# One pass over the sample states, row scaling on ScalarE and a norm on 8 partitions at the end of a gated delta rule

## The reference

```
a_mat = strict_lower((k*beta) k^T * decay);  t_mat = inverse(I + a_mat)
w_v   = t_mat (v*beta);   w_k = t_mat (k*beta*exp(gc))
v_new = w_v - w_k S                       # per chunk, S is the state
o     = (q*exp(gc)) S + (q k^T * decay) v_new
S     = S*g_last + (k*exp(gc_last-gc))^T v_new
o_b   = rms_norm(o, o_norm_w) * silu(g_b)
out   = concat(o_a, o_b) w_out            # 288 tokens x 1024, weights 1024 x 1024
```

## Time and profile before

| | |
|---|---|
| median of 3 runs | 1420.63 us (1409.93 to 1421.68) |
| profiled execution, its own time | 1418.56 us |
| its span, mean granted TensorE clock | 1416.9 us, 0.855 |
| PE busy / DVE / ACT / POOL | 1134.4 / 413.6 / 215.0 / 87.6 us |
| inverse, seven levels | 372.7 to 420.6 us |
| scaling to the last head's output | 420.6 to 485.7 us |
| projection, norm and state update | 485.8 to 541.6 us |
| write of the sample states (L1504) | 2048 KB |

### The profile page before, as it was taken

One profiled execution on the slowest core, in us unless ns is written; L12 is line 12 of the kernel. 1 busy time (PEld: TensorE's weight loads), 2 busy tenths in 40 slices (PEclk: granted clock), 3 DMA queues, 4 the chain that ended last, 5 costly groups with the idle time before them and its releaser, 6 DMA issues. The chain is left out here.

```text
span 1416.9 us, 15651 instructions
## 1 busy us (share of the span) xinstructions
PE 1134.4 (80%) x6028; PEld 611.0 (43%) x6028; DVE 413.6 (29%) x1016; ACT 215.0 (15%) x445; POOL 87.6 (6%) x189
## 2 busy tenths in 40 slices
PE   1999987777778997778788665999999687887755
PEld 0877656564777733325233112444444324222211
DVE  1342234333682243421122113023201521122204
ACT  2221122422000101011011002113101111010001
POOL 6331030040000000000000000000000000000000
PEclk9999968898895577687999877999999688798878
DMA  9251271783600034089999996343423249999991
GB/s 281 69 159 54 60 241 31 212 268 138 251 1 0 1 126 178 1 355 405 397 384 395 392 356 209 105 133 119 156 89 133 105 189 387 420 411 420 383 374 45
DMA packets 87711, 298.73 MB, mean 211 GB/s; under 512 B 16067, under 2 KB 52475, under 8 KB 57902
## 3 DMA queue, kind: packets, MB, share of 16 engines
q1 hardware_dynamic: 67760, 272.91, 50.1%
q0 software_dynamic: 5152, 17.05, 3.9%
q10 hardware_dynamic: 14718, 7.69, 2.0%
HBM read 292.46 MB, written 5.16 MB: 210 GB/s over the span
## 5 line engine op out<-in xcount | busy, mean ns | idle before, releaser
L1052 PE MATMUL ps<-arena,hT 128*32 128x512 f32 x1024 | 142.8, 712 | 93.8 <-DMA arena<-in_moe_w_up 61.1
L1052 PEld LDWEIGHTS ps<-arena,hT 128*32 128x32 f32 x1024 | 38.5, 127 | 187.1 <-issue 187.1
L646 PE MATMUL ps<-hT,arena 128*128 128x288 f32 x448 | 115.2, 420 | 0.0
L1220 PE MATMUL ps<-arena,hT 128*128 128x512 f32 x256 | 114.2, 607 | 0.9 <-ACT hT L1368 0.9
L646 PEld LDWEIGHTS ps<-hT,arena 128*128 128x128 f32 x448 | 87.5, 197 | 27.3 <-issue 1.7
L1220 PEld LDWEIGHTS ps<-arena,hT 128*128 128x128 f32 x256 | 49.5, 195 | 62.7 <-issue 62.6
L2150 DVE TENSOR_TENSOR arena<-ps,arena 128x256 f32<-128x256 f32 x16 | 6.8, 424 | 215.1 <-ACT arena L1551 215.1
L1011 PE MATMUL ps<-htok,arena 128*128 128x512 f32 (+1 forms) x96 | 63.4, 796 | 0.0
L1077 PE MATMUL ps<-arena 128*32 128x512 f32 x512 | 58.2, 595 | 3.3 <-ACT arena L1556 3.3
L1310 PE MATMUL ps<-arena 128*128 128x512 f32 x128 | 59.2, 605 | 0.0
L596 PE MATMUL ps<-ident,htok 128*128 128x128 f32 (+1 forms) x48 | 13.8, 401 | 43.5 <-DVE htok L1654 43.5
(11 more groups left out here) (463 smaller groups left out, 1491.0 us busy)
## 6 DMA issues: line engine op xcount, KB each, us to landing
arena<-in_moe_w_gate SPq DMA_DIRECT2D x66, 1024.0 KB, 12.0
arena<-in_moe_w_up SPq DMA_DIRECT2D x66, 1024.0 KB, 13.2
arena<-in_moe_w_down SPq DMA_DIRECT2D x66, 1024.0 KB, 16.4
arena<-in_cache_k SPq DMA_DIRECT2D x64, 256.0 KB, 3.3
arena<-in_cache_v POOLq DMA_DIRECT2D x64, 256.0 KB, 3.3
arena<-in_w_in_odd SPq DMA_DIRECT2D x16, 1024.0 KB, 10.4
arena<-in_w_in_even SPq DMA_DIRECT2D x14, 1024.0 KB, 10.6
arena<-in_w_out_odd SPq DMA_DIRECT2D x8, 1024.0 KB, 7.0
```

Of the source, the lines that this page charges most:

```text
L646: last = mm(ps[:, c % 4, 0:T], w[:, k, P * (c % 2):P * (c % 2 + 1)], hT[:, k, :], start=k == 0, stop=k == KD - 1)
L1052: last = mm(ps[EC * j:EC * (j + 1), q % 2, :], xgT[:, k, GC * p + EC * j:GC * p + EC * (j + 1)], ring[:, 2 * j:2 * j + 2, DE * k:DE * (k + ...
L1220: last = mm(ps[:, bank, :], hT[:, k, P * i:P * (i + 1)], ring[:, 2 * n:2 * n + 2, QC * k:QC * (k + 1)], start=k == 0, stop=k == KD - 1)
```

## The change

- The last inverse level leaves out the correction of `dT`.
- The row scalings go to ACT, as copies of 128x128 with a scale per row, issued behind its exponentials while the inverse runs; `bex` is made by VectorE ahead of the decay multiplies; buffers `kbe` and `vb` move (v is scaled in place).
- The products with T of tile i write banks 2i and 2i+1; VectorE evicts the first, ACT the second. For the sample tile ACT writes its 4 columns per sample into `wq`, where VectorE puts the decayed q beside them.
- One pass over S0 with 8 columns (`from_states`, bank 5) in two halves of two heads, placed between the steps of the prompt's state chain. Its first 4 columns correct v, the other 4 are added to `oT` by VectorE before the square.
- The heads' prompt part (`o_prompt`) and sample part (`o_sample`) are separate; the transposes of the correction stand between them.
- The sums of squares go to 8 partitions (through `osel`), ACT's root and VectorE's reciprocal work on 8x288, and a product with a column of the identity spreads each head's row to 128 partitions; gate, norm weight and o are multiplied before that.
- `out_proj(j, c)` is one channel block, half of a pair; sums, broadcasts and state products stand between the halves.

```diff
@@ -198,7 +198,10 @@
...
 vdt = htok[:, :, 512:1024].rearrange("p t (h e) -> p t h e", h=HB)
-kbe, vb, wkT, wv = dU, dMT, dT, dLT
+vb, wkT, wv = vdt, dT, dLT
+kbe = wk(4096, 3, HB, P)
+osr = wk(4096, T)
+wq = wk(5632, HB, NB, 2 * QS)
 osq = wk(A + 6144, HB, T)
@@ -604,21 +607,21 @@
...
-    def out_proj(part):
-        for j in part:
+    def out_proj(j, c):
+        if c == 0:
             wait_even(pe, 14 + j)
-            w = cview(14 + j)
...
-                              start=(j == 0 and c == 0), stop=(j == 3 and c == 1))
+        w = cview(14 + j)
+        for i in range(2):
+            for hf in range(2):
+                mm(ps[:, 2 * i + hf, :], mixT[:, 2 * j + c, P * i:P * (i + 1)],
+                   w[:, c, 512 * hf:512 * (hf + 1)],
+                   start=(j == 0 and c == 0), stop=(j == 3 and c == 1))
+        for qr in range(4):
+            last = mm(ps[TS * qr:TS * (qr + 1), 4, 0:QC], mixT[:, 2 * j + c, TP:T],
+                      w[:, c, QC * qr:QC * (qr + 1)],
+                      start=(j == 0 and c == 0), stop=(j == 3 and c == 1))
+        if c == 1:
             last.then_inc(s.w_used, 1)
@@ -862,85 +865,109 @@
...
             for h in range(HB):
-                mm(inv_ps(i, 1)[:, h, :], dTT[0:m, i, h, 0:m], dU[0:m, i, h, 0:m], start=True, stop=True)
+                if l < 6:
+                    mm(inv_ps(i, 1)[:, h, :], dTT[0:m, i, h, 0:m], dU[0:m, i, h, 0:m], start=True, stop=True)
             for h in range(HB):
...
     pe.wait_ge(s.dl_scaled, 2)
-    pe.wait_ge(s.dl_t, 1 + 2 * inv_no(6, 1))
+    pe.wait_ge(s.dl_t, 3 + 2 * inv_no(5, 1))
     for i, (r0, m) in enumerate(TOK):
-        if i:
-            pe.wait_ge(s.dl_w, 2 * i)
         for h in range(HB):
-            mm(ps[0:m, 0, P * h:P * (h + 1)], dTT[0:m, i, h, 0:m], vb[0:m, i, h, :], start=True, stop=True)
+            mm(ps[0:m, 2 * i, P * h:P * (h + 1)], dTT[0:m, i, h, 0:m], vb[0:m, i, h, :], start=True, stop=True)
         for h in range(HB):
-            last = mm(ps[:, 1, P * h:P * h + m], kbe[0:m, i, h, :], dTT[0:m, i, h, 0:m], start=True, stop=True)
+            last = mm(ps[:, 2 * i + 1, P * h:P * h + m], kbe[0:m, i, h, :], dTT[0:m, i, h, 0:m], start=True, stop=True)
         last.then_inc(s.dl_w_ps, 1)
...
+    def state_step(i, bank):
+        for h in range(HB):
+            last = mm(ps[:, bank, P * h:P * (h + 1)], kdt[:, i, h, :], wv[:, i, h, :], start=True, stop=True)
+        last.then_inc(s.dl_s_ps, 1)
+    def from_states(heads):
+        for h in heads:
+            for b in range(NB):
+                last = mm(ps[:, 5, 64 * h + 8 * b:64 * h + 8 * (b + 1)], S0[:, HB * b + h, :], wq[:, h, b, :],
+                          start=True, stop=True)
+        return last
     pe.wait_ge(s.dl_w, 6)
+    state_step(0, 2)
     pe.wait_ge(s.dl_qdec, 1)
-    for h in range(HB):
-        last = mm(ps[:, 2, P * h:P * (h + 1)], kdt[:, 0, h, :], wv[:, 0, h, :], start=True, stop=True)
-    last.then_inc(s.dl_s_ps, 1)
+    pe.wait_ge(s.s0_loaded, 16)
+    from_states((0, 1))
     pe.wait_ge(s.dl_s, 1)
...
     last.then_inc(s.dl_s_ps, 1)
+    from_states((2, 3)).then_inc(s.dl_s_ps, 1)
     pe.wait_ge(s.dl_s, 2)
-    for h in range(HB):
...
-    for h in range(HB):
+    state_step(1, 2)
+    def o_prompt(h):
         b = ps[:, 6 + h % 2, :]
...
             pe.wait_ge(s.dl_o, h - 1)
-        for i, (r0, m) in enumerate(TOK):
-            mm(b[:, r0:r0 + m], wv[0:m, i, h, :], dQK[0:m, i, h, 0:m], start=(i == 0), stop=False,
+        for i in range(2):
+            mm(b[:, P * i:P * (i + 1)], wv[:, i, h, :], dQK[:, i, h, :], start=(i == 0), stop=False,
                skip_group_check=True)
         mm(b[:, P:TP], Sp[:, 0, h, :], cv[:, h, P:TP], start=False, stop=False, skip_group_check=True)
-        for q in range(NB):
...
-    pe.wait_ge(s.dl_osq, 1)
+    def o_sample(h):
+        mm(ps[:, 6 + h % 2, TP:T], wv[0:TS, 2, h, :], dQK[0:TS, 2, h, 0:TS], start=False, stop=True,
+           skip_group_check=True).then_inc(s.dl_o_ps, 1)
+    o_prompt(0)
+    pe.wait_ge(s.dl_s, 3)
     for h in range(HB):
-        if h >= 2:
...
-    pe.wait_ge(s.dl_orms, HB)
+        last = tr(ps[0:TS, 4, P * h:P * (h + 1)], vsT[:, TS * h:TS * (h + 1)], ident[:, :])
+    last.then_inc(s.dl_s_ps, 1)
+    o_prompt(1)
+    pe.wait_ge(s.dl_s, 4)
+    o_sample(0)
+    o_sample(1)
+    for h in (2, 3):
+        o_prompt(h)
+        o_sample(h)
+    def broadcast(h):
+        mm(ps[:, (5, 6, 7, 5)[h], 0:T], bc(ident[0:8, h:h + 1], [8, P]), osr[0:8, :], start=True,
+           stop=True).then_inc(s.dl_oss_ps, 1)
     vx = vexp.rearrange("p b (h e) -> p b h e", h=HB)
-    for j in range(8):
+    def state_change(j):
         h, q = j // 2, j % 2
...
            stop=True).then_inc(s.dl_su_ps, 1)
+    pe.wait_ge(s.dl_st_out, 1)
+    out_proj(0, 0)
+    pe.wait_ge(s.dl_osq, 1)
+    for h in range(HB):
+        last = mm(ps[0:8, 6, 0:T], osel[:, 7 - h:15 - h], osq[:, h, :], start=h == 0, stop=h == HB - 1)
+    last.then_inc(s.dl_oss_ps, 1)
+    out_proj(0, 1)
+    out_proj(1, 0)
+    pe.wait_ge(s.dl_orms, 2)
+    for h in range(3):
+        broadcast(h)
+    out_proj(1, 1)
+    pe.wait_ge(s.dl_mixed, 3)
+    broadcast(3)
+    pe.wait_ge(s.dl_vexp, NB)
+    state_change(0)
+    state_change(1)
     pe.wait_ge(s.dl_mixed, HB)
-    pe.wait_ge(s.dl_su, 8)
-    pe.wait_ge(s.dl_o, HB)
-    out_proj((2, 3))
+    for n in range(4):
+        out_proj(2 + n // 2, n % 2)
+        if n < 3:
+            state_change(2 * n + 2)
+            state_change(2 * n + 3)
@@ -1489,15 +1516,33 @@
...
         A_(dDT[0:m, i, :, 0:m], dDT[0:m, i, :, 0:m], ACT.Exp).then_inc(s.dl_dtx, 1)
+    act.wait_ge(s.dl_scaled, 1)
+    for i in range(3):
+        m = TOK[i][1]
+        for h in range(HB):
+            A_(kbe[0:m, i, h, :], kdt[0:m, i, h, :], ACT.Copy, scale=bex[0:m, i, h:h + 1])
+            A_(vb[0:m, i, h, :], vb[0:m, i, h, :], ACT.Copy, scale=beta[0:m, i, h:h + 1])
+    act.wait_ge(s.dl_cols, 2)
+    for i in range(3):
+        m = TOK[i][1]
+        for h in range(HB):
+            last = A_(kdt[0:m, i, h, :], kdt[0:m, i, h, :], ACT.Copy, scale=kdc[0:m, i, h:h + 1])
+    last.then_inc(s.dl_scaled, 1)
+    for i in range(3):
+        act.wait_ge(s.dl_w_ps, i + 1)
+        src = ps[:, 2 * i + 1, :].rearrange("p (h c) -> p h c", h=HB)
+        if i < 2:
+            A_(wkT[:, i], src, ACT.Copy).then_inc(s.dl_w, 1)
+        else:
+            A_(wq[:, :, :, 0:QS], src[:, :, 0:TS].rearrange("p h (b q) -> p h b q", q=QS), ACT.Copy).then_inc(s.dl_w, 1)
...
         A_(oT[:, h, :], ps[:, 6 + h % 2, 0:T], ACT.Copy).then_inc(s.dl_o, 1)
-    act.wait_ge(s.dl_o, HB)
+    act.wait_ge(s.dl_o, HB + 1)
     A_(osq[:, :, :], oT[:, :, :], ACT.Square).then_inc(s.dl_osq, 1)
-    for h in range(HB):
-        act.wait_ge(s.dl_oss_ps, h + 1)
-        A_(osq[:, h, :], ps[:, 6 + h % 2, 0:T], ACT.Sqrt, scale=1.0 / DB, bias=epsb).then_inc(s.dl_orms, 1)
+    act.wait_ge(s.dl_oss_ps, 1)
+    A_(osr[0:8, :], ps[0:8, 6, 0:T], ACT.Sqrt, scale=1.0 / DB, bias=epsb[0:8]).then_inc(s.dl_orms, 1)
     act.wait_ge(s.dl_st_out, 1)
@@ -1839,6 +1884,8 @@
...
                                    ).then_inc(s.dl_dt, 1)
+    dve.wait_ge(s.dl_cols, 2)
+    V.tensor_tensor(bex, beta, egc, ALU.mult).then_inc(s.dl_scaled, 1)
     for i in range(3):
@@ -1874,50 +1921,38 @@
...
             dve.wait_ge(s.dl_t_ps, inv_no(l, i))
-            V.tensor_tensor(dT[0:m, i, :, 0:m], dT[0:m, i, :, 0:m], inv_ps(i, 1), ALU.subtract)\
-                .then_inc(s.dl_t, 1)
+            if l < 6:
+                V.tensor_tensor(dT[0:m, i, :, 0:m], dT[0:m, i, :, 0:m], inv_ps(i, 1), ALU.subtract)\
+                    .then_inc(s.dl_t, 1)
             V.tensor_tensor(dTT[0:m, i, :, 0:m], dTT[0:m, i, :, 0:m], inv_ps(i, 2), ALU.subtract)\
                 .then_inc(s.dl_t, 1)
-    dve.wait_ge(s.dl_t, 1 + 2 * inv_no(6, 1))
...
-    last.then_inc(s.dl_qdec, 1)
+    dve.wait_ge(s.dl_t, 3 + 2 * inv_no(5, 1))
+    for i in range(2):
+        V.tensor_tensor(cv[:, 0:HB, P * i:P * (i + 1)], cv[:, 0:HB, P * i:P * (i + 1)], eR[:, i], ALU.mult)
+    V.tensor_tensor(wq[:, :, :, QS:2 * QS], cv[:, 0:HB, TP:T].rearrange("p h (b q) -> p h b q", q=QS),
+                    eR[:, 2, :, 0:TS].rearrange("p h (b q) -> p h b q", q=QS), ALU.mult).then_inc(s.dl_qdec, 1)
+    hv = lambda b: ps[:, b, :].rearrange("p (h c) -> p h c", h=HB)
     for i in range(3):
...
         dve.wait_ge(s.dl_w_ps, i + 1)
-        V.tensor_copy(wv[0:m, i], ps[0:m, 0, :].rearrange("p (h c) -> p h c", h=HB)).then_inc(s.dl_w, 1)
...
-    hv = lambda b: ps[:, b, :].rearrange("p (h c) -> p h c", h=HB)
+        V.tensor_copy(wv[0:m, i], hv(2 * i)[0:m]).then_inc(s.dl_w, 1)
+    sq = ps[:, 5, 0:256].rearrange("p (h b c) -> p h b c", h=HB, b=NB)
     dve.wait_ge(s.dl_s_ps, 1)
...
     V.tensor_tensor(wv[:, 1], wv[:, 1], hv(3), ALU.subtract).then_inc(s.dl_s, 1)
+    dve.wait_ge(s.dl_s_ps, 3)
+    V.tensor_copy(vsT.rearrange("p (h b c) -> p h b c", h=HB, b=NB), sq[:, :, :, 0:QS]).then_inc(s.dl_s, 1)
```

(65 more changed lines are left out.)

22 lines of the change are left out of this document (removed).

## The result

The changed kernel takes 1375.18 us in the median of four runs (1365.18 to 1380.79) where the kernel before took 1421.16 beside it (1409.93 to 1428.41): ratio 0.9688, with an interval of 0.9623 to 0.9754. The profiled execution took 1376.67 us, its span is 1375.1, its mean granted clock 0.871. Ratios leave out runs over 1.5% slower than the fastest of their kernel, medians are over all runs. Run again with the first experiments the same program took 1380.34 us in the median where the kernel before took 1418.96, ratio 0.9783 (0.9743 to 0.9822): the two intervals barely meet, so the whole time alone says only that 2 to 4% are gained.

What follows compares the result with a forecast made beforehand. TensorE, waiting in turn with VectorE and often at half clock, was taken as the path before a transfer-bound expert stage. Gains summed to 46.2 us: 1418.56 - 46.2 = 1372.4 for the profiled execution, 1374 for the median, range 1362 to 1389.

Steps and rivals of the forecast that it cites:

- The bound: Expert stage behind the change is transfer-bound but starts when its input is there; a microsecond saved before 541 us reaches the end.
- Inverse and scaling: Last inverse level and row scalings: products with T begin at 418.4 in place of 426.8, gain 8.4 us.
- The forecast's 418.3: Time in us when the last inverse level is ready, after VectorE's scaling, about 1.0 us of products and one subtraction.
- Products with T: Own banks and a shared eviction cut 13.4 us to 5.45 at full clock, gain 7.9, or 3.4 at half clock.
- State chain and heads: State chain up to the projection: gain 4.1 us in the chain and 15.2 in the output heads.
- Half clock in the pass: Pass over the states priced at clock 0.50, 6.9 us per half; chain gain 4.1 us, against 13.3 at full clock.
- rival b: Full clock throughout: projection starts at 439, gain 56 us, time 1364; chance 15%.
- The rise within the heads: Dense 128-column passes raise the clock within the output heads: 7 us, against 8.9 at half clock.
- rival a: Half clock up to the projection, which starts at 457.2: gain 38 us, time 1383, with further stalls 1389; chance 27%.
- Projection: Projection, norm and state update: halves of 4.2 us, 0.7 us wait before the sums, end at 495.2 against 541.6.
- the prediction's own signs: Among them: projection about 45 us, started 36 us earlier; wrong if its halves don't follow each other at 4.2 us.
- Rivals c and d: c: expert stage absorbs the gain, 1407 to 1420, 5%; d: state write delays the router, 1435, 3%.

Runs made afterwards that it cites:

- pad64: Changed kernel with 64 columns instead of 8 in the products with the sample states; state chain and heads 23.4 us against 24.8, ratio 0.9719 to the kernel before.
- Pad128: Changed kernel with 128 columns instead of 8 in the products with the sample states; state chain and heads 16.9 us against 24.8, ratio 0.9707 to the kernel before.
- late_decay: Changed kernel with VectorE's decay of the states moved behind the product with the gate; projection 47.05 us, 1.3 less.

## Why the prediction was right

*The bound.* That a microsecond saved before the router is one at the end held: the part behind the projection is as long as before in all traces (869 to 878 us), and moved as a block. The loads of the down weights left at 512.8, 8.9 us behind the projection, against 4.2 before: SP did wait for the later write of the states (issued at 500.4, so it took at most 12.3 us), and it cost nothing: the router's first instruction follows the projection by 21.0 us before and 21.1 after.

*Inverse and scaling*, forecast 8.4, measured 7.3, and 8.3 from the last level's first pass to the products with T (12.25 us before, 3.94 after); the missing microsecond is the clock in the inverse's first level. The forecast's 418.3 holds 0.2 us beyond the terms that it names (416.4, 1.0 and 0.68 make 418.1); the trace has that step at 1.95 us, so they were there. ACT's 36 copies took 10.6 us from 366.9, the lower bound, and were done 46 us before they were needed.

*Products with T*, forecast 7.9, measured 6.8. The third tile's 32-row passes took 2.1 us at full clock, not 1.0: I had halved them with their rows, but 8 of them take 1.05 us where 8 passes with 128 rows take 1.06.

*State chain and heads*, forecast 19.3, measured 20.8. Half clock in the pass, my choice between the two prices, was right: 6.56 and 6.83 us against the forecast 6.9 twice, and of rival b's 3.5 nothing was seen. The Trainium skill's page "TensorE: Matmul & The Clock Gate", section "Why this matters for your kernels", would have had the full clock for a TensorE kept continuously busy; the windows from 436 to 448 us and pad64's disagree. Pad128's from 442 to 448 us agrees, but not the 4 us ahead of it, also busy throughout, at 0.56 to 0.59. The rise within the heads came as forecast (four passes of L914 took 1.06 us for the first two heads and 0.71 for the others). By the positions of the kernel before, the projection started at 450.9, where the forecast had 450.2, rival a 457.2 and rival b 439. The price of the heads at half clock, 8.9, has a slip of 0.2 (four times 2.1 and 0.3), which the forecast did not use.

*Projection*, forecast 10.8, measured 7.4: the term that was mis-sized. The wait ahead of the sums of squares was 1.2 us and not 0.7, a clock dip at the first pair of state products cost 1.7 (5.40 for a half in place of 3.70), and sums, broadcasts and pairs of state products took 1.1 more than their columns. late_decay shows the first; the halves of 3.70 us at the same place in other traces show the second. Why the clock dips there in some traces and not in others was not tried. I had named the dip only as a part of rival a. By the prediction's own signs this is its weak part: one of the eight halves is followed after 5.9 us and not 4.2, and the stretch is 48.4 and not near 45; the other signs came, near enough (its start 34.9 us earlier, not 36).

What each edit is worth, from undoing it alone in the changed kernel: the second pass 13.4, the state products between the halves 5.6, the scalings on ACT 5.1 (7.8 in the first two lengths), the pass between the chain's steps 1.8 in the sum (2.7 to 3.0 in its own stretch), the banks 0.9 (1.9 in its stretch), the norm -2.2 (-1.4 against projections without a dip). These don't add up to 42.4, since edits share waits and clock; what is left, above all the engine of the second eviction, the last level's product and the split heads, was not tried by itself. Rivals c and d are out: no stage took the gain back, and the state write did not reach the router.

## What to carry to other kernels

A long vector instruction under enough matrix work cost nothing here, and replacing it by short ones plus products on the bounding engine cost what those products take: ask for the cover first, as with the reciprocal of 7.35 us. In a stretch bound by weight loads more columns cost nothing, up to the 128 tried here, and filling them out to 128 brought the full clock back within the pass: 9.1 us in place of 13.4. In a kernel whose whole time scatters by more than the edit, measure the edit's own stretch in the trace, between two instructions that both programs have.
